# Hybrid block kernel: the first attention block in another order of slabs, x rows loaded later to a place of their own, more warm-up matmuls

## The reference

```python
h = rms_norm(x, norm1_g)
proj = h @ w_in          # 8 retention heads: q, k, v, gate; 8 attention heads: q, k, v
ret = silu(rg) * head_group_norm(retention(rotary(rq), rotary(rk), rv))
att = chunk_attention(rms_norm(aq, q_norm_g), rms_norm(ak, k_norm_g), av, rel_bias)
x = x + concat([ret, att]) @ w_out
h = rms_norm(x, norm2_g)
x = x + square(relu(h @ w_ff1)) @ w_ff2
```

## Time and profile before

| | |
|---|---|
| median of 3 runs | 1110.92 us (1110.43 to 1111.0) |
| the profiled execution | 1109.77 us |
| its span, first to last instruction | 1108.0 us |
| TensorE busy | 1100.2 us, 99% |
| TensorE weight loads busy | 932.8 us, 84% |
| VectorE busy | 879.8 us, 79% |
| ScalarE busy | 695.0 us, 63% |
| GpSimd busy | 54.3 us, 5% |
| DMA, mean | 238 GB/s |

### The profile page before, as it was taken

The page is one execution under the profiler, slowest core; times in us unless marked ns, Lnnn a source line. Parts: engine busy times, 40 slices in busy tenths (PEclk is TensorE's granted clock), DMA queues, the critical chain, the costliest instruction groups (busy, mean ns, idle before and its releaser), DMA issues.

```text
span 1108.0 us, 13182 instructions
## 1 busy us (share of the span) xinstructions
PE 1100.2 (99%) x5186; PEld 932.8 (84%) x5186; DVE 879.8 (79%) x871; ACT 695.0 (63%) x823; POOL 54.3 (5%) x69
## 2 busy tenths in 40 slices
PE   9999999999999999999999999999999999999998
PEld 9789989989988888888888888888888888888887
DVE  7878868868868678869787869787869787869784
ACT  7774674674674555677655577655577665577662
POOL 0100100100100000000000000000000000000000
PEclk9999999999999999999999999999999999999999
DMA  9875675675686557787787787787787797787792
GB/s 358 264 266 185 175 272 183 176 274 175 179 290 230 198 192 189 265 284 215 241 291 223 257 281 216 245 288 224 259 278 219 247 290 219 261 280 217 246 279 91
DMA packets 43966, 263.81 MB, mean 238 GB/s; under 512 B 4864, under 2 KB 7680, under 8 KB 16256
## 3 DMA queue, kind: packets, MB, share of 16 engines
q1 hardware_dynamic: 37712, 220.61, 53.5%
q0 software_dynamic: 5760, 41.95, 20.3%
q10 hardware_dynamic: 432, 0.41, 0.1%
HBM read 260.85 MB, written 2.10 MB: 237 GB/s over the span
## 4 chain that ended last, share of the span: by engine, by line
PE 95%; DMA 2%; DVE 2%; SPq 0%; POOL 0%; issue 0%; ACT 0%; DVEq 0%
PE acc L910 10%; PE acc L912 10%; PE acc L914 10%; PE acc L781 7%; PE acc L794 7%; PE acc L788 7%; PE bankC L872 4%; PE acc L865 4%; PE bankC L865 4%; PE bankC L867 4%; PE acc L867 4%; PE acc L872 4%; PE acc L609 2%; PE acc L614 2%; PE acc L621 2%; DMA raw<-in_w_att 2%
## 5 line engine op out<-in xcount | busy, mean ns | idle before, releaser
L1750 DVE TENSOR_TENSOR w_lo<-raw,w_hi 128x2048 fp32r<-128x2048 f32 x180 | 410.6, 2287 | 126.9 <-ACT w_hi L1272 126.6
L1272 ACT ACTIVATE w_hi<-raw 128x2048 fp32r<-128x2048 f32 x180 | 344.7, 1916 | 219.9 <-PE acc L914 147.0
L1469 DVE TENSOR_TENSOR w_lo<-raw,w_hi 128x1024 fp32r<-128x1024 f32 (+1 forms) x150 | 163.8, 1107 | 39.5 <-ACT w_hi L1036 39.4
L1036 ACT ACTIVATE w_hi<-raw 128x1024 fp32r<-128x1024 f32 (+1 forms) x150 | 140.5, 966 | 21.0 <-DVE raw L1478 14.0
L781 PE MATMUL acc<-w_hi,hT_hi 128*128 128x384 f32 (+1 forms) x408 | 104.5, 374 | 0.9 <-ACT w_hi L1036 0.8
L910 PE MATMUL acc<-w_hi,hF_hi 128*128 128x512 f32 x256 | 100.8, 394 | 0.0
L914 PE MATMUL acc<-w_hi,hF_lo 128*128 128x512 f32 x256 | 99.8, 390 | 0.0
L912 PE MATMUL acc<-w_lo,hF_hi 128*128 128x512 f32 x256 | 99.6, 389 | 0.0
L794 PE MATMUL acc<-w_lo,hT_hi 128*128 128x384 f32 (+1 forms) x408 | 97.4, 356 | 0.6 <-DVE w_lo L1469 0.6
L788 PE MATMUL acc<-w_hi,hT_lo 128*128 128x384 f32 (+1 forms) x408 | 97.7, 357 | 0.0
L910 PE MATMUL acc<-w_hi,dF_hi 128*128 128x512 f32 x248 | 96.8, 390 | 0.0
(11 more groups left out here) (272 smaller groups left out, 1826.8 us busy)
## 6 DMA issues: line engine op xcount, KB each, us to landing
raw<-in_w_up SPq DMA_DIRECT2D x64, 1024.0 KB, 6.0
raw<-in_w_down SPq DMA_DIRECT2D x64, 1024.0 KB, 6.3
raw<-in_w_ret SPq DMA_DIRECT2D x32, 1024.0 KB, 5.5
raw<-in_w_att SPq DMA_DIRECT2D x28, 768.0 KB, 4.2
raw<-in_w_out SPq DMA_DIRECT2D x16, 1024.0 KB, 4.8
raw<-in_w_up POOLq DMA_DIRECT2D x16, 1024.0 KB, 8.8
raw<-in_w_down POOLq DMA_DIRECT2D x16, 1024.0 KB, 8.9
raw<-in_w_ret POOLq DMA_DIRECT2D x8, 1024.0 KB, 9.0
```

Of the source, the lines that this page charges most:

```text
L1036: nc.scalar.activation(piece(w_hi, q, 0, n), raw[:, r, half * n:(half + 1) * n], ACT.Copy).then_inc(hi_done, 1)
L1272: nc.scalar.activation(w_hi[:, ring(s)], raw[:, r, :], ACT.Copy).then_inc(slab_hi, 1)
L1469: nc.vector.tensor_tensor(piece(w_lo, q, 0, n), raw[:, IN_PLAN[i, READ_AT.get(step, step)][0], half * n:(half + 1) * n], piece(w_hi, q, 0, ...
L1750: nc.vector.tensor_tensor(w_lo[:, ring(s)], raw[:, r, :], w_hi[:, ring(s)].bitcast(f32), ALU.subtract).then_inc(slab_lo, 1)
```

## The change

In the first block alone:

- The heads take turns: I0 J0 I1 J1 I2 Q1 J2 P5 I3 P6 J3, then as before. Now I2 is pieces 8 and 9, Q1 10 and 11, J2 12 and 13, P5 14 and 15, I3 16 and 17, P6 18 and 19, J3 20 and 21. The loads follow, with x pieces 4 to 7 later in the queue, and x pieces are split at the pieces in X_AT.
- The rows of x go to four buffers `xq` of their own, and are loaded behind slab b and around I3.
- All eight sums of squares are on ScalarE, in pieces 12 to 15 (two of the eight were on VectorE); `x_mean_squares` is at piece 15 of VectorE, ahead of the sum of a and d.
- Head I is evacuated at piece 18 into a buffer `ap_first`; its jobs on TensorE move from 14, 16, 20, 22 to 23, 25, 27, 28, and those of head J from 27, 28, 31, 33 to 30, 31, 33, 34.
- 12 warm-up matmuls instead of 7.

```diff
@@ -42,13 +42,17 @@
 SLOTS = 4
 AHEAD = 2
 OUT_GROUPS = D_MODEL // N
-WARM_UP = 7
+WARM_UP = 12
 FINE = 2
 FF_ROUNDS = D_FF // D_MODEL
 BLOCKS = HEADS // 2
-STEPS = "I0 I1 I2 I3 J0 Q1 J1 P5 J2 P6 J3 P7 P3 Z1 Q2 Z2 P4 H1 H2".split()
-LOADS = "I0 I1 I2 I3 J0 a b J1 J2 d J3 Z1 e Z2 H1 H2".split()
-IN_PIECES = 2 * len(STEPS)
+STEPS = ["I0 J0 I1 J1 I2 Q1 J2 P5 I3 P6 J3 P7 P3 Z1 Q2 Z2 P4 H1 H2".split()] + [
+    "I0 I1 I2 I3 J0 Q1 J1 P5 J2 P6 J3 P7 P3 Z1 Q2 Z2 P4 H1 H2".split()] * (BLOCKS - 1)
+LOADS = ["I0 J0 I1 J1 I2 a J2 b I3 d J3 Z1 e Z2 H1 H2".split()] + [
+    "I0 I1 I2 I3 J0 a b J1 J2 d J3 Z1 e Z2 H1 H2".split()] * (BLOCKS - 1)
+LEAD = LOADS[0][:SLABS]
+X_AT = {2: 2, 3: 3, 8: 4, 9: 5, 14: 6, 15: 7}
+IN_PIECES = 2 * len(STEPS[0])
 G_OUT = BLOCKS * IN_PIECES // PIECES
 RET_ORDER = [h + 1 - 2 * (h % 2) for h in range(HEADS)]
...
+        xq = [at(f"xq{c}", (68, 72, 84, 88)[c], [P, MT, N]) for c in range(OUT_GROUPS)]
...
-            for q in range(FINE, PIECES):
+
+            def load_x(q):
                 s, o = q // 2, q % 2
                 sp.dma_start(xc[s][:, o * half_x:(o + 1) * half_x],
                              x_pieces[:, q * half_x:(q + 1) * half_x]).then_inc(xc_in[q], 16)
-                sp.dma_start(raw[:, s, o * half_w:(o + 1) * half_w],
-                             w_att[s * P:(s + 1) * P, o * half_w:(o + 1) * half_w]).then_inc(
-                                 slab_in[s] if o else half_in[s], 16)
-
+
+            for s in range(1, SLABS):
+                row = ((LEAD[s][0] == "J") * SLABS + int(LEAD[s][1])) * P
+                for o in range(2):
+                    sp.dma_start(raw[:, s, o * half_w:(o + 1) * half_w],
+                                 w_att[row:row + P, o * half_w:(o + 1) * half_w]).then_inc(
+                                     slab_in[s] if o else half_in[s], 16)
+                    if s == 1:
+                        load_x(2 + o)
+            load_x(4)
+            load_x(5)
+            for name in ("I2", "a", "J2"):
+                load_in(0, name)
+            load_x(6)
+            load_x(7)
+            load_in(0, "b")
             x_rows = x.rearrange("b (m p) d -> p (b m) d", p=P)
             for c in range(OUT_GROUPS):
-                sp.dma_start(xs[:, :, c * N:(c + 1) * N], x_rows[:, :, c * N:(c + 1) * N]).then_inc(x_in[c], 16)
+                sp.dma_start(xq[c][:], x_rows[:, :, c * N:(c + 1) * N]).then_inc(x_in[c], 16)
                 if c == 0:
-                    load_in(0, "J0")
-            for name in LOADS[5:8]:
-                load_in(0, name)
-            load_in(0, LOADS[8])
+                    load_in(0, "I3")
+            load_in(0, "d")
+            load_in(0, "J3")
             load_bias(0)
-            for name in LOADS[9:11]:
-                load_in(0, name)
...
-                if i == 0 and step[0] == "I":
-                    pe.wait_ge(xc_hi, 2 * q + 2)
+                if i == 0 and step[0] in "IJ":
+                    pe.wait_ge(xc_hi, SLAB_KT * int(step[1]) + 2 * half + 2)
...
-                for h, places in ((2 * i, (13, 15, 20, 22) if i else (14, 16, 20, 22)), (2 * i + 1, (27, 28, 31, 33))):
+                for h, places in ((2 * i, (13, 15, 20, 22) if i else (23, 25, 27, 28)),
+                                  (2 * i + 1, (27, 28, 31, 33) if i else (30, 31, 33, 34))):
...
+                if h == 0:
+                    act.wait_ge(xc_lo, 3 * SLAB_KT)
...
-                act.wait_ge(ms_ok, 1)
...
+            def x_squares(c):
+                act.wait_ge(x_in[c], 16)
+                for m in range(MT):
+                    squares(m, c, xq[c][:, m, :], ss, MT * c + m)
...
-            at_piece(0, 5, x_squares_first)
-            at_piece(0, PIECES - 1, x_squares)
-            for f, pos in enumerate((9, 10, 13, 14)):
+            for f, pos in enumerate((9, 11, 18, 20)):
                 at_piece(0, pos, s_hi, f)
+            for c, pos in enumerate((12, 13, 14, 15)):
+                at_piece(0, pos, x_squares, c)
             for i in range(BLOCKS):
                 h, u, late = 2 * i, 2 * i, i == BLOCKS - 1
...
+                if i == 0:
+                    at_piece(i, 12, keep_in_q1, i)
+                    at_piece(i, 16, keep_in_p5, i)
+                    at_piece(i, 18, att_proj, h)
+                    at_piece(i, 19, att_squares, h)
+                    at_piece(i, 22, att_proj, h + 1)
+                    at_piece(i, 23, att_qT, h)
+                    at_piece(i, 24, set_y, i)
+                    at_piece(i, 25, set_h, i)
+                    at_piece(i, 25, att_squares, h + 1)
+                    at_piece(i, 26, att_exp, h)
+                    at_piece(i, 27, att_pT, h)
+                    at_piece(i, 28, att_mix, h)
+                    at_piece(i, 30, att_qT, h + 1)
+                    at_piece(i, 32, att_exp, h + 1)
+                    at_piece(i, 32, ret_proj, u)
+                    at_piece(i, 33, att_pT, h + 1)
+                    at_piece(i, 34, att_mix, h + 1)
...
-                if nxt < PIECES:
-                    x_hi(nxt)
+                if nxt in X_AT:
+                    x_hi(X_AT[nxt])
...
             def x_mean_squares():
-                for c in range(2, OUT_GROUPS):
-                    dve.wait_ge(x_in[c], 16)
-                    cols = xs[:, 1, c * N:(c + 1) * N]
-                    nc.vector.tensor_tensor_reduce(rp[:, c % MT, :], cols, cols, 1.0 / D_MODEL, 0.0,
-                                                   ALU.mult, ALU.add, ss[:, 1, c:c + 1]).then_inc(squared_dve, 1)
-                dve.wait_ge(squared_dve, OUT_GROUPS - 2)
-                dve.wait_ge(squared, MT + OUT_GROUPS)
+                dve.wait_ge(squared, MT * OUT_GROUPS)
                 nc.vector.tensor_reduce(ms[:], ss[:], AX.X, ALU.add).then_inc(ms_ok, 1)
...
+                    at_piece(i, 11, in_sum, i, "b", "Q1")
+                    at_piece(i, 15, x_mean_squares)
+                    at_piece(i, 15, in_sum, i, "d", "P5")
+                    at_piece(i, 20, set_z, i)
+                    at_piece(i, 20, att_mean_squares, h)
+                    at_piece(i, 21, att_norm, h)
+                    at_piece(i, 23, set_w, i)
+                    at_piece(i, 25, att_bias_max, h)
+                    at_piece(i, 26, att_probs, h)
+                    at_piece(i, 27, att_mean_squares, h + 1)
+                    at_piece(i, 28, att_mix, h)
+                    at_piece(i, 28, att_norm, h + 1)
+                    at_piece(i, 31, att_bias_max, h + 1)
+                    at_piece(i, 32, att_probs, h + 1)
+                    at_piece(i, 33, ret_rotate, u)
+                    at_piece(i, 34, att_mix, h + 1)
...
```

More of the change, by code:

```diff
@@ L365, in in_plan @@
             for i in range(BLOCKS):
-                for name in LOADS:
+                for name in LOADS[i]:
                     r = min(free, key=lambda r: free[r])
-                    if i > 0 or name[0] != "I":
+                    if i > 0 or name not in LEAD:
                         uses[r] += 1
@@ L378, in in_step @@
             s, half = divmod(q, 2)
-            i, n = divmod(s, len(STEPS))
-            return i, STEPS[n], half
+            i, n = divmod(s, len(STEPS[0]))
+            return i, STEPS[i][n], half
         def in_cols(step):
@@ L493, in _ @@
             load_decay(1)
-            for name in LOADS[11:]:
+            for name in LOADS[0][11:]:
                 load_in(0, name)
             for i in range(1, BLOCKS):
-                for name in LOADS:
+                for name in LOADS[i]:
                     load_in(i, name)
@@ L661, in att_pv @@
                 pe.wait_ge(a_pT_ok, h + 1)
-                nc.tensor.matmul(bankA[:, 0:SEQ], ap_[:, 0, 2 * HD:3 * HD], a_pT[:, 0:SEQ], start=True, stop=False)
-                nc.tensor.matmul(bankA[:, P:SEQ], ap_[:, 1, 2 * HD:3 * HD], a_pT[:, SEQ:SEQ + P],
+                v = [att_rows(h)[:, m, 2 * HD:3 * HD] for m in range(MT)]
+                nc.tensor.matmul(bankA[:, 0:SEQ], v[0], a_pT[:, 0:SEQ], start=True, stop=False)
+                nc.tensor.matmul(bankA[:, P:SEQ], v[1], a_pT[:, SEQ:SEQ + P],
                                  start=False, stop=True).then_inc(a_pv, 1)
@@ L782, in in_piece @@
                                          start=fresh, stop=False, skip_group_check=True)
-                if i == 0 and step[0] == "I":
-                    pe.wait_ge(xc_lo, 2 * q + 2)
+                if i == 0 and step[0] in "IJ":
+                    pe.wait_ge(xc_lo, SLAB_KT * int(step[1]) + 2 * half + 2)
                 for bank, m in banks:
@@ L1020, in in_hi @@
                 r, loaded, _ = IN_PLAN[i, READ_AT.get(step, step)]
-                if i == 0 and step[0] == "I":
+                if i == 0 and step in LEAD:
                     act.wait_ge(slab_in[q // 2] if half else half_in[q // 2], 16)
@@ L1176, in _, with squares @@
                                      ACT.Copy).then_inc(hi_done if t % 2 else tile_hi, 1)
-            def squares(m, c, sums, before, spare=junk[:]):
```

(36 more changed lines are left out.)

82 lines of the change are left out of this document (33 added, 49 removed).

## The result

| | before | after |
|---|---|---|
| median of 10 runs each | 1110.15 us (1109.68 to 1111.0) | 1112.75 us (1111.87 to 1114.31) |
| ratio to before, 95% interval | | 1.0025, 1.0017 to 1.0033 |
| the profiled execution | 1109.77 us | 1112.32 us |
| its span | 1108.0 us | 1110.5 us |
| TensorE busy | 1100.2 us | 1099.5 us |

What follows compares the result with a forecast made beforehand. TensorE bounds the kernel, losing 5.4 us before P7. Block 1 at 56.4 + 37.86 + 1.05 + 0.3 + 0.1 + 0.85 = 96.6 us, 2.6 later, less 0.2 for an early start: +2.4, 1113.3 us; range 1109.0 to 1115.8.

Steps and rivals of the forecast that it cites:

- about the same: Rival: start gives 1.2 us, add lands in 8.7, head 1's wait is covered; +1.2 us, 1112.1; chance 0.37.
- The start: TensorE's warm-up: twelve matmuls raise the clock by their end, so piece 2 starts at 11.2 us, 1.0 earlier.
- the bound of 11.0: Piece 2's earliest start, limited by x tiles' landing near 9.3 us and ScalarE's w_hi: 9.3 + 0.9 + 0.84.
- The loads: Loads in the new order at 391 GB/s: none late, pieces 2 to 9 without a wait, piece 9 at 28.1 us.
- The squares: ScalarE's row with eight squares takes 10.7 us, to 42.9; sum follows mean, TensorE stands 3.0 us ahead of P6.
- The add: GpSimd's DMA onto slab b waits for mean and power: issued 44.5, landed 53.5 us, P7 at 56.4.
- Both chains end together: Ahead of P7, ScalarE's chain ends at 56.1 and the add's at 56.4 us; curing one would give 0.3.
- Both heads late: Behind P7's start: head 0's jobs 1.05 us, three stream breaks of 0.1, att_T 0.1, head 1's new wait 0.85.
- PT's wait: Ahead of head 1's PT: chain of 3.95 us against 3.1 of TensorE work, a new wait of 0.85 us.
- The sum: All terms added: block 1's first piece at 96.6 us instead of 93.96; +2.4 forecast after the early start bound.
- Faster: Rival: squares don't hold P6 and P7; block 1 at 89.8, 4.2 us sooner, 1106.7 us; chance 0.15.
- Slower by more: Rival: clock rises at 10.4 us as now (+4.1, 1115.0) or add takes 10.9 us (+4.5, 1115.4); chance 0.12.

Runs made afterwards that it cites:

- the early sum: Changed kernel with VectorE's sum of slabs a and d moved ahead of the mean, nothing else; 1114.93 us, ratio 1.0044.
- the few squares: Changed kernel squaring only the first quarter of x's columns, so the mean is of that quarter; 1111.16 us, ratio 1.0011.
- The kernel with the add moved: Changed kernel with GpSimd's adding DMA onto slab b issued ahead of the mean and power; 1111.55 us, ratio 1.0013.
- the last kernel: Mended kernel with head I's small squares behind w_hi 22 and head J's jobs up to its probabilities one piece sooner; 1107.33 us, ratio 0.9976.
- both cures: Changed kernel with the sum of a and d ahead of the mean and GpSimd's add ahead of the power; 1108.76 us, ratio 0.9988.
- mended: Changed kernel with squares split between ScalarE and VectorE, add ahead of power, sum ahead of mean, s_hi and s_third made earlier; 1108.48 us, ratio 0.9985.

## Why the prediction was right

The forecast was +2.4 us on the median; measured were +2.6 (1110.15 to 1112.75). The absolute 1113.3 is 0.55 too high, since it was counted from the median of the three runs then known, and before's further runs lay lower. The forecast's own chance was only 0.36, against 0.37 for "about the same"; the measured interval, 0.17% to 0.33%, reaches under the 0.2% that parts the two. So the side on which the result fell was nearly even odds; the path to it was right.

- **The start.** Piece 2 at 11.24, forecast 11.2, and tile matmuls at the fast pace from about 7. But the step that gave the credit to the twelve warm-ups was not shown: with seven the changed kernel got there as early. And 11.24 to the tenth is luck: with the same start other executions had piece 2 at 10.38 to 11.58, the first below the bound of 11.0 that the prediction took from the data.
- **The loads.** No wait up to Q1, piece 9 used at 28.0, forecast 28.1. Right.
- **The squares.** ScalarE's row ran from 32.28 to 42.51, 10.2 us of a forecast 10.7. TensorE stood 3.0 us ahead of P6 from start to start (the matmuls of I3 from 39.10 fill 4.16), as forecast. Shown by the early sum and by the few squares, which both moved P6 by 2.5 to 3.0 us.
- **The add.** The path was right, and its end is luck in part: two errors cancel. The power took 2.63 us, not the 1.02 of the earlier trace rows, so the issue came at 45.67 instead of 44.5; the landing took 8.0, less than any of before's eight, so the data came at 53.67 instead of 53.5. P7 then at 56.76, forecast 56.4.
- **Both chains end together.** Forecast 0.3 us apart, measured 0.68 (ScalarE's own chain would have had P7 at 56.76 - 0.68 = 56.08, forecast 56.1). The kernel with the add moved started P7 at 55.98. "Curing one would give 0.3 us" was right in kind, and the pair of experiments with both shows that it holds from either side.
- **Both heads late.** From P7 to block 1 39.97 us against 37.86, 2.11 more where the terms made 2.3. The mis-sized one is PT's wait, 0.70 for 0.85. Half of the 2.11 is head I's work that stood ahead of P7 before. Only PT's wait was put to the test, in the last kernel: with it gone and one of 0.47 in its place, P7 to block 1 is 39.69.
- **The sum.** Block 1 at 96.73, forecast 96.6.

The rivals. "About the same" came close: its landing of 8.7 us was even 8.0, but the power took that back, the start gave 1.0 and not 1.2, and head J's wait of 0.70 was covered by nothing. "Faster" needed the squares through by 40.3 and P7 at 53.8; with both cures P7 stood at 53.65 and the kernel came out 0.12% faster, with its squares as late as ever. So the turning point of P7 was right, and that of the squares was one way to it, not the only one. "Slower by more" by a late clock at the start did not come; that the clock could fall in mid-block, behind the very waits that I forecast, was in none of the rivals.

Of the two levels of TensorE's clock the Trainium skill (TensorE: Matmul & The Clock Gate, Part 1) says that activity releases the throttle and idleness brings it back. The rows behind the waits of 2.8, 3.3 and 5.0 us agree; those behind 1.7 (both) and 1.6 us (mended) show no loss.

## What to carry to other kernels

When two chains end within a microsecond of each other, test the cures in pairs: here one alone brought P7 0.8 us forward, the other made the whole run 2.2 us slower, and both together made it 4 us faster, all against the changed kernel. Before a reduction is moved later because its engine has time there, look for what hangs on its result on other engines' queues, above all a DMA issued behind it in program order. And price a wait of TensorE not by its length alone: one of 2.8 us cost 1.4 more for the clock here.
